# Gathering the later experts' rows with indirect transfers and combining the outputs in two one-pass products, in a two-layer encoder with 8 routed experts

## The reference

```python
logits = t @ w_router
top_vals, top_idx = lax.top_k(logits, 2)
top_w = softmax(top_vals)
combine = sum(one_hot(top_idx, 8) * top_w[..., None], axis=1)
for e in range(8):
    y = (silu(t @ w_gate[e]) * (t @ w_up[e])) @ w_down[e]   # 1024 -> 3584 -> 1024
    out = out + combine[:, e:e+1] * y
```

## Time and profile before

| | |
|---|---|
| median of 3 runs | 1826.73 us |
| the profiled execution, its own time | 1823.88 us |
| its span, first to last instruction | 1822.0 us |
| outside the span | 1.88 us |
| TensorE / VectorE / ScalarE / GpSimd busy | 97% / 77% / 65% / 1% of the span |
| the seven gathers of the loop, start of the first and of the last | 918.8 us, 1670.1 us |
| the experts, first product of step 0 to last down product | 807.9 us to 1807.0 us |

### The profile page before, as it was taken

How to read it: one execution, slowest core, us unless ns; L and a number is a source line. 1 busy time by engine, 2 the same in 40 slices (tenths; PEclk the granted TensorE clock), 3 DMA queues, 4 the chain that set the end, 5 groups by cost and what they waited for, 6 DMA issues and landing times.

```text
span 1822.0 us, 23915 instructions
## 1 busy us (share of the span) xinstructions
PE 1768.2 (97%) x8356; PEld 1449.6 (80%) x8356; DVE 1406.3 (77%) x1382; ACT 1177.0 (65%) x1242; POOL 20.2 (1%) x20
## 2 busy tenths in 40 slices
PE   7999999999999999989999999999999999999997
PEld 6777878888887778777888878878878888788785
DVE  7776876544577678769888889888888888898884
ACT  7555665434466556557777767677777777777772
POOL 0200000000002000000000000000000000000000
PEclk9999999999999999989999999999999999999999
DMA  7433345555454333668989989999999899899980
GB/s 278 162 116 116 116 155 188 189 185 185 157 196 139 116 128 127 259 251 342 374 333 358 370 318 371 349 341 378 344 346 372 329 362 366 322 371 346 343 323 25
DMA packets 67129, 475.79 MB, mean 261 GB/s; under 512 B 7793, under 2 KB 8049, under 8 KB 9969
## 3 DMA queue, kind: packets, MB, share of 16 engines
q1 hardware_dynamic: 67056, 474.86, 69.5%
HBM read 473.78 MB, written 1.05 MB: 261 GB/s over the span
## 4 chain that ended last, share of the span: by engine, by line
PE 87%; DVE 5%; ACT 3%; issue 1%; DVEq 1%; ACTq 1%; DMA 1%; SPq 0%
PE ps_proj L938 11%; PE ps_proj L942 11%; PE ps_proj L941 11%; PE ps_proj L538 7%; PE ps_proj L540 7%; PE ps_proj L541 7%; PE ps_score L938 6%; PE ps_score L941 6%; PE ps_score L942 6%; PE ps_ctx L532 3%; PE ps_score L532 2%; PE ps_trans L569 2%; PE ps_trans L532 1%; PE ps_score L538 1%; PE ps_score L541 1%
## 5 line engine op out<-in xcount | busy, mean ns | idle before, releaser
L2138 DVE TENSOR_TENSOR w_raw_r<-w_raw,hi 128x2048 fp32r<-128x2048 f32 x336 | 759.8, 2289 | 123.7 <-ACT hi L1450 107.5
L1450 ACT ACTIVATE hi<-w_raw 128x2048 fp32r<-128x2048 f32 x335 | 640.0, 1918 | 200.3 <-PE ps_score L942 77.7
L938 PE MATMUL ps_proj<-hi,he_hi 128*128 128x512 f32 x896 | 357.0, 398 | 0.6 <-DVE w_raw_r L2138 0.3
L942 PE MATMUL ps_proj<-w_raw_r,he_hi 128*128 128x512 f32 x896 | 349.4, 390 | 0.0
L941 PE MATMUL ps_proj<-hi,he_lo 128*128 128x512 f32 x896 | 349.2, 390 | 0.0
L1071 ACT ACTIVATE hi<-raw 128x2048 fp32r<-128x2048 f32 (+1 forms) x114 | 215.8, 1893 | 124.4 <-PE ps_proj L540 60.7
L1562 DVE TENSOR_TENSOR raw_r<-raw,hi 128x2048 fp32r<-128x2048 f32 (+1 forms) x114 | 257.1, 2265 | 34.2 <-ACT hi L1071 27.0
L538 PE MATMUL ps_proj<-hi,hT_hi 128*128 128x512 f32 (+2 forms) x496 | 198.7, 401 | 6.3 <-DVEq L1548 4.0
L938 PEld LDWEIGHTS ps_proj<-hi,he_hi 128*128 128x128 f32 x896 | 168.3, 188 | 36.4 <-issue 2.6
L942 PEld LDWEIGHTS ps_proj<-w_raw_r,he_hi 128*128 128x128 f32 x896 | 168.2, 188 | 36.2
L941 PEld LDWEIGHTS ps_proj<-hi,he_lo 128*128 128x128 f32 x896 | 168.5, 188 | 34.9 <-issue 1.7
(11 more groups left out here) (331 smaller groups left out, 2010.1 us busy)
## 6 DMA issues: line engine op xcount, KB each, us to landing
w_raw<-in_w_exp SPq DMA_DIRECT2D x336, 1024.0 KB, 4.8
raw<-in_w_pre SPq DMA_DIRECT2D x110, 1024.0 KB, 4.9
raw<-in_w_pre SPq DMA_DIRECT2D x4, 640.0 KB, 6.0
x_tok<-in_x_rows SPq DMA_DIRECT2D x2, 512.0 KB, 5.2
raw<-in_w_pre SPq DMA_DIRECT2D x2, 512.0 KB, 6.2
out_rows<-x_tok SPq DMA_DIRECT2D x1, 1024.0 KB, 4.7
grow<-in_ffn_row SPq DMA_DIRECT2D x1, 512.0 KB, 5.7
cst<-in_const SPq DMA_DIRECT2D x1, 344.0 KB, 8.5
```

Source lines behind the costliest of these rows:

```text
L938: m = nc.tensor.matmul(o, a_hi, w_h, start=first, stop=False)
L942: return nc.tensor.matmul(o, a_hi, w_l, start=False, stop=last)
L1450: A(w_hi[k % HS][:], w_raw[n], ACT.Copy).then_inc(gran_hi, 1)
L2138: V.tensor_tensor(w_low[k % WS], w_raw[k % WS], w_hi[k % HS][:].bitcast(F32), ALU.subtract)\
```

## The change

- The first expert's rows are gathered by products as before. SyncE also stores `htok` to a memory tensor `h_rows` (1 MB). For experts 1 to 7 GpSimd fetches 128 rows of 4 KB by an indirect transfer into `herow`, and TensorE transposes them (8 transposes, `turn_rows`) in step 6.
- The row numbers and weights by slot come from a new small product (`slot_columns`): `G` with `pair`, the weight and the row number of each token (2 columns, 2 float32 products). VectorE copies them to `idx` and `w_next`. It is done in step 4 for the next expert, and for the first expert after its step 0.
- The weight is applied to the expert's output: ScalarE writes `y_hi`, scaled and rounded to float32r, VectorE writes `y_lo`, the rest (`low_outputs`, in step 8 after the first `low`). `S` is now the transpose of `G`, in float32r. The combine is two float32r products, high and low, in place of one float32 product.
- `Gw` is gone; `one_weight` copies two columns instead.

SyncE:

```diff
+            sp.wait_ge(htok_ready, TT)
+            sp.dma_start(h_rows.rearrange("(t p) d -> p t d", p=P), htok[:]).then_inc(rows_stored, 16)
```

TensorE:

```diff
+            def turn_rows(number, bank_value):
+                pe.wait_ge(herow_in, number)
+                for half, bank in enumerate(("ctx", "trans1")):
+                    o = take(bank, bank_value(bank))
+                    for b in range(4):
+                        c = (half * 4 + b) * P
+                        m = nc.tensor.transpose(o[:, b * CAP:(b + 1) * CAP], herow[:, c:c + P], c_("ident"))
+                    m.then_inc(full[bank], 1)
+            def slot_columns(ready, value):
                 pe.wait_ge(weights_ready, ready)
                 o = take("proj2", value)
                 for t in range(TT):
+                    m = mm(o[:, 0:2], G[:, t], pair[:, t], t, TT)
+                m.then_inc(full["proj2"], 1)
+            def scatter_matrix(value):
+                o = take("proj2", value)
+                for t in range(TT):
-                    m = nc.tensor.transpose(o[:, t * P:(t + 1) * P], Gw[:, t], c_("ident"))
+                    m = nc.tensor.transpose(o[:, t * P:(t + 1) * P], G[:, t], c_("ident"))
                 m.then_inc(full["proj2"], 1)
             def combine(t, bank_value):
                 for half, bank in enumerate(("ctx", "trans1")):
                     o = take(bank, bank_value(bank))
-                    mm(o[:], S[:, t * P:(t + 1) * P], yrow[:, half * 512:(half + 1) * 512], 0, 1)\
-                        .then_inc(full[bank], 1)
+                    for n, y in enumerate((y_hi, y_lo)):
+                        m = mm(o[:], S[:, t * P:(t + 1) * P], y[:, half * 512:(half + 1) * 512], n, 2)
+                    m.then_inc(full[bank], 1)
...
+                    if s == 4 and not isinstance(e, int):
+                        slot_columns(along(2, rnd, EXPERTS, e, 1), bank_use("proj2", 2, rnd, e))
                     project(0, s, e)
...
                     if s == EXP_CHUNKS - 1 and not isinstance(e, int):
-                        gather(along(2, rnd, EXPERTS, e, 1), lambda bank: bank_use(bank, 1, rnd, e))
+                        turn_rows(along(16, rnd, 16 * EXPERTS, e, 16), lambda bank: bank_use(bank, 1, rnd, e))
...
                 step(0, 0)
+                if first_round(rnd):
+                    first_columns()
-                scatter_matrix(along(1, rnd, EXPERTS), bank_use("proj2", 0, rnd))
+                scatter_matrix(bank_use("proj2", 1, rnd))
                 step(1, 0)
```

ScalarE, in `outputs`:

```diff
-                        m = A(yrow[:, b * 512:(b + 1) * 512], o[:], ACT.Copy)
-                        if b:
-                            m.then_inc(y_ready, 1)
-                        act.drain().then_inc(free[f"score{b}"], 1)
+                        A(y_hi[:, b * 512:(b + 1) * 512], o[:], ACT.Identity, scale=w_now[:, 0:1])\
+                            .then_inc(y_hi_ready, 1)
```

VectorE:

```diff
             def one_weight(e):
                 for t in range(TT):
-                    m = V.tensor_scalar(Gw[:, t], c_("slot_no"), slots_of[:, t, bass.ds(e, 1)],
-                                        wt[:, t, bass.ds(e, 1)], ALU.is_equal, ALU.mult)
+                    m = V.tensor_copy(pair[:, t, 0:1], wt[:, t, bass.ds(e, 1)])
                 m.then_inc(weights_ready, 1)
+            def slot_columns(value):
+                o = fresh("proj2", value)
+                V.tensor_copy(idx[:], o[:, 1:2]).then_inc(idx_ready, 1)
+                V.tensor_copy(w_next[:], o[:, 0:1])
+                dve.drain().then_inc(free["proj2"], 1)
+            def weights_on():
+                V.tensor_copy(w_now[:], w_next[:])
+                dve.drain()
+            def low_outputs(number):
+                for b in range(2):
+                    dve.wait_ge(y_hi_ready, number(b + 1))
+                    half = slice(b * 512, (b + 1) * 512)
+                    m = V.scalar_tensor_tensor(y_lo[:, half], ps[f"score{b}"][:], w_now[:, 0:1],
+                                               y_hi[:, half].bitcast(F32), ALU.mult, ALU.subtract)
+                    if b:
+                        m.then_inc(y_ready, 1)
+                    dve.drain().then_inc(free[f"score{b}"], 1)
...
                     if s:
                         low(down0, e)
+                    if s == EXP_CHUNKS + 1:
+                        low_outputs(lambda n: along(n, rnd, 2 * EXPERTS, e, 2))
+                        weights_on()
+                    if s:
                         low(down0 + 1, e)
...
                     low(next0 + 1, e)
+                    if s == 4 and not isinstance(e, int):
+                        slot_columns(bank_use("proj2", 2, rnd, e))
...
                 step(0, 0)
+                if first_round(rnd):
+                    slot_columns(bank_use("proj2", 0, rnd))
+                    weights_on()
+                    dve.wait_ge(rows_stored, 16)
                 step(1, 0)
...
                 turned(EXP_CHUNKS - 1, last)
+                low_outputs(lambda n: along(n, rnd, 2 * EXPERTS, last, 2))
```

GpSimd:

```diff
+            def gather_rows(rnd, e):
+                pool.wait_ge(idx_ready, along(1, rnd, EXPERTS, e, 1))
+                pool.wait_ge(he_ready, along(0, rnd, 2 * EXPERTS, e, 2))
+                G_.indirect_dma_start(herow[:], None, h_rows, bass.IndirectOffsetOnAxis(ap=idx[:, 0:1], axis=0))\
+                    .then_inc(herow_in, 16)
+            pool.wait_ge(rows_stored, 16)
+            for e in range(1, EXPERTS):
+                gather_rows(0, e)
```

More of the change, by code:

```diff
@@ L48 @@
 CONST, CONST_COLS = columns(("ident", P), ("slope", HEADS), ("inv_freq", HALF), ("rope_g", DEPTH * 2 * ROPE),
-                            ("before", P), ("ones", P), ("slot_no", CAP), ("first_wins", EXPERTS))
+                            ("before", P), ("ones", P), ("slot_no", CAP), ("first_wins", EXPERTS), ("row_no", TT))
 GAIN, GAIN_COLS = columns(("attn", DB), ("ffn", DB), ("q_lat", QLB), ("kv_lat", KLB), ("qn", 1), ("kn", 1),
@@ L199, in first_gran @@
     return 6 * s - 2 if s else 0
-MOE_USES = dict(ctx=(24, 3), trans1=(24, 3), proj2=(8, 1), score0=(8, 1), score1=(8, 1))
+MOE_USES = dict(ctx=(24, 3), trans1=(24, 3), proj2=(16, 2), score0=(8, 1), score1=(8, 1))
 def bank_use(bank, k, rnd, e=0):
@@ L210, with build @@
 SBUF_AT = 16512
-def build(nc, x_rows, pos_row, pos_col, const, gains, lam_vecs, w_pre, ffn_row, w_router, w_exp, out):
+def build(nc, x_rows, pos_row, pos_col, const, gains, lam_vecs, w_pre, ffn_row, w_router, w_exp, out, h_rows):
     with ExitStack() as ctx:
@@ L303, in build @@
         grow = place("grow", [D], base + 32 * K)
-        yrow = place("yrow", [D], base + 32 * K)
+        y_hi = place("y_hi", [D], base + 32 * K, F32R)
         he_hi, he_lo = (place(n, [DB, CAP], base + at * K, F32R) for n, at in (("he_hi", 84), ("he_lo", 88)))
@@ L906, in route, with gather @@
                 mm(o[:, 2 * E:4 * E], ranks[:, 1], selb[:, 0:2 * E], 0, 1).then_inc(full["proj2"], 1)
-            def gather(value, bank_value):
+            def gather(bank_value):
                 pe.wait_ge(htok_ready, TT)
-                pe.wait_ge(gather_ready, value)
+                pe.wait_ge(gather_ready, 1)
                 for half, bank in enumerate(("ctx", "trans1")):
@@ L1493, in step @@
                     if s == EXP_CHUNKS + 1:
-                        scatter_matrix(bank_use("proj2", 1, rnd, e))
+                        scatter_matrix(bank_use("proj2", 3, rnd, e))
                     if s == EXP_CHUNKS - 1:
@@ L1504, in experts @@
                 step(0, 0)
-                scatter_matrix(bank_use("proj2", 0, rnd))
+                scatter_matrix(bank_use("proj2", 1, rnd))
                 step(1, 0)
@@ L2249, in _ @@
                 m.then_inc(rotated_q, 1)
+            def gather_rows(rnd, e):
[6 more added lines that the diff above has]
+                gather_rows(0, e)
+            pool.wait_ge(rounds_ready, 1)
+            n = pool.value_load(nrnd[0:1, 0:1], min_val=1, max_val=MAX_ROUNDS)
+            with pool.If(n > 1):
+                with pool.Fori(1, n) as rnd:
+                    for e in range(EXPERTS):
+                        gather_rows(rnd, e)
 def constants(f):
@@ L2347 @@
     out = nc.dram_tensor("out_rows", (T, D), F32, kind="ExternalOutput").ap()
-    build(nc, *args, out)
+    h_rows = nc.dram_tensor("h_rows", (T, D), F32).ap()
+    build(nc, *args, out, h_rows)
     r = run_bass_kernel_spmd(nc, [arrays], core_ids=[0])
```

31 lines of the change are left out of this document (25 added, 6 removed).

## The result

The changed kernel takes **1804.84 us** (median of 4 runs, 1804.76 to 1806.92); the kernel before beside it took 1826.50 us (4 runs, 1824.71 to 1827.22). The ratio is 0.9883, 95% interval 0.9871 to 0.9894: faster by 21.7 us. The forecast was 1811.5 us with a range of 1803.5 to 1821.5 us, of which 1806 to 1817 us was the forecast's own.

What follows compares the result with a forecast made beforehand. The prediction took TensorE to set the experts' time. Its terms summed to -15.2 us from the profiled 1823.88 us, giving 1808.7, plus 2.85 to the median: 1811.5 us, range 1803.5 to 1821.5 us (its own 1806 to 1817).

Steps and rivals of the forecast that it cites:

- The gather: In step 6 of the loop, eight transposes replace 32 instructions: 2.68 us gained, 7 times, -18.8 us.
- The combine: In step 8, four one-pass products per combine gain 0.81 us, 14 times in the loop: -11.3 us.
- Step 8's waits: TensorE's second combine waits for two banks that VectorE frees late: 0.7 us, 7 times, +4.9 us.
- Step 6: The shorter turn brings the next expert's gate product nearer to `he_lo`: +0.7 us for seven (0 to 3).
- The first expert's start: Between steps 0 and 1 TensorE waits 7.7 us for VectorE to read the columns, then half clock: +5.9 us.
- The end: After the last expert, y comes 1.0 us later and the last addition ends 0.3 us later: +0.3 us.
- What is hidden: The 1 MB store and the indirect transfers cost no time; the fetched rows have 33.7 us of cover.
- From execution to median: 2.85 us added, because the median of the runs stood that far above the profiled execution.
- (a): Milder handovers: no step 8 wait, no fall of the clock, no wait in step 6; 1804.3 us, 12%.
- (b): VectorE is held up 1.5 us more per expert beside GpSimd, in steps 4 and 5; 1822.0 us, 14%.
- (c): The combine's two products are not one-pass and gain nothing: 11.3 us more, 1822.8 us, 3%.
- (d): Indirect rows land after TensorE wants them in `turn_rows`; each microsecond beyond the cover costs 7; slower, 7%.

Runs made afterwards that it cites:

- e1: Changed kernel with the eight transposes of fetched rows made eight float32 products, each issued twice, the transfer kept: 1824.59 us, ratio 0.9997.
- e2: Changed kernel with the old float32 combine, without the second product and `low_outputs`: 1813.84 us, ratio 0.9935.
- e7: Changed kernel with `combined(0)` ahead of `low(next0+1)` in VectorE's step 8: 1802.71 us, ratio 0.9858.
- e3: Changed kernel with the first expert's columns moved behind step 1, so nothing waits for bank proj2: 1802.48 us, ratio 0.9872.
- e10: The kernel before, unedited, in one more profiled execution: 1829.02 us.
- e11: The changed kernel, unedited, run again: 1806.69 us, ratio 0.9878.
- e5: Changed kernel with the columns and the indirect transfer moved from step 4 to step 6 of each expert: 1854.85 us, ratio 1.0148.
- e6: Changed kernel with the columns and the indirect transfer moved from step 4 to step 5: 1805.20 us, ratio 0.9881.
- e9: The kernel before with one edit, VectorE's `turned(0)` two weight granules earlier in step 1: 1823.17 us, ratio 0.9975.
- e8: Changed kernel with the first expert's columns behind step 1, `combined(0)` earlier and `turned(0)` two granules earlier: 1795.10 us, ratio 0.9820.

## Why the prediction was right, step by step

The time lay 6.7 us under the forecast: in the stated range, 1.3 us above its lower end, but under the 1806 us where the forecast's own range began. So what was right is the mechanism and most of the terms. The sum's terms against what was measured:

- **The gather**, -2.68 us an expert: -2.70, and e1 gives it back (19.8 us with its noise, for 18.8). Right.
- **The combine**, -0.81 us: -0.79 for the first of the two; together with step 8's wait 6.4 us net were predicted, and e2's loop gives back 7.7.
- **The columns**, +0.45 us: 0.45 (877.48 to 878.16 us less one interval). Right.
- **Step 8's waits** were in the right place (bank trans1, VectorE late by its own order) and mis-sized: 0.7 us an expert was said, the holes come to 0.53 and 0.54 is what e7 wins back. The outputs' operations took 0.75 us as taken from the earlier trace rows.
- **Step 6**: 0.1 us an expert was said. The period leaves 0.05 for it: 2.70 + 0.79 + 0.26 - 0.45 is 3.30, measured 3.25. No run tried it alone.
- Together the loop gained 23.0 us where 21.4 were predicted.
- **The first expert's start**, +5.9 us: +5.3. The wait was 7.28 us for 7.7 predicted and the lost clock 1.4 for 1.6. The reading that a stand after small products is nearer to the earlier trace rows's half rate than to the 3.1 us that left the clock alone was right. What it took from those rows was too much, though: e3 and e10 show that the 3.1 us wait is no safe length. In e1, e2 and e11 the clock behind the 7.3 us wait cost about 3 us, in e5, e6 and e7 1.4 to 1.7, so the term is 5 to 7 us from run to run.
- **The end**, +0.3 us: +0.7; the second pair ran at half clock.
- **What is hidden** stayed hidden: TensorE waits neither for the store nor for a transfer, and the cover is 33.8 us (index read at 889.12 us, rows turned at 922.93) for 33.7 predicted. The full rate of 385 GB/s was read too low: stretches of 2 us show 418 GB/s, and 422 in the changed kernel; nothing hung on it.
- **From execution to median**, +2.85 us: this term missed most, and its reason was wrong. The prediction added to its forecast what the median of before stood above its profiled execution. The profiled kernel before was a lucky one, which kept its clock at two places where e10 lost 2.9 us each. The changed kernel has no clock to lose at 831 us, because its longer wait took that loss into the first expert's term; its median stands 0.1 us over its profiled execution. So the offset was in part added on top of a loss already counted. Only in part: the place at 178 us lies ahead of the experts and is left in both kernels, and in e11's series the changed kernel's median is 1806.69 us, 1.9 above that first profiled execution. How much of the 2.8 us is the chance of four runs is open.
- The rest of the miss lies outside the change: 1.5 us before step 0, which is chance, and 0.7 behind the last addition.

In sum the misses are 2.8 + 1.5 + 0.6 + 1.6 - 0.4 + 0.7 = 6.8 us (offset, before step 0, first expert, loop, end, behind the end; 6.7 unrounded).

**The rivals.** (a) named nearly the measured time, 1804.3 us, by a mechanism that didn't happen: the clock fell and the second combine waited. (b) did not happen: `low` takes 2290 ns on average as before, at most 2337, and GpSimd's instruction 0.94 us in six of seven cases (the first 2.69). (c) is out by the pitch of 0.23 us. (d) has its condition far off: the rows land 6.8 to 10.8 us after the issue, and the 33 us of cover are three times that. Its price of 7 us for each microsecond of lateness left out the clock: e5 pays 14 us of lost clock beside 33.0 us of stands. The Trainium skill's lock of GpSimd's descriptor writes by VectorE (SBUF — State Buffer, the "DVE blocks DMA" trap) is told there of VectorE's operations in a 2-port mode, such as copies of float32 within SBUF. This case does not test it: from 1000 to 1050 us VectorE is busy 43.4 us, and 39.5 of them are subtractions of two tensors. Beside these no transfer of the changed kernel took longer than 10.8 us. The 2.69 us of the first one is no such hold by what the runs show: it is 2.69 us in all ten traces with indirect transfers, also where e5 and e6 issue it at another time, and 0.94 in every later pass at the same place of the loop.

## What to carry to other kernels

Where one engine's instructions set the time, a change there is worth its pitch times its count, and the rest of the answer is which bank or buffer the shortened work now reaches too soon: here three handovers mended by the order of the work alone gave 9.7 us more. Not all of it is what the change gave back: the wait for `turned(0)` stood in the kernel before as well, and mended there alone (e9) it is worth 4.5 us. With that mend on both sides, and its own two handovers mended, the change is worth 28.1 us (e9 to e8), where it brought 21.7. A bank that the bound engine uses twice in a row, with a busy engine's read in between, is such a handover; put a step of work between the two uses (e3 moves the columns behind step 1), or the read ahead of a granule (e7). Before adding the distance between one profiled execution and the median to a forecast, look at where the clock fell in that execution: one trace is one draw of every such place.

## What the hardware showed unexpectedly

- The same wait of 3.1 us for the same instruction left the clock at 1.00 in one execution of the kernel before and at 0.50 in another (e10), and in e3. Behind it TensorE worked about 6 us at half rate, 2.9 us lost. A wait of 3.3 us at 178 us, in the attention, which neither the change nor an edit touches, stands in all thirteen traces: four kept the clock behind it, nine lost 1.4 to 3.0 us.
- How long the half rate lasts behind the same wait of 7.3 us differs too: 1.4 us lost in the changed kernel, 3.0 in e11, the same kernel.
- Of the differences between runs of one kernel a large part is this: 6.3 us more lost clock came with a span 5.2 us longer. Less its lost clock, the kernel before has spans of 1816.9 and 1815.8 us (e10), and the changed kernel, which lost 7.6 and 9.9 us, of 1795.3 and 1795.8 us (e11): what the change is worth, 20.0 to 21.6 us, does not hang on that draw. What decides the draw was not tried.
- An indirect transfer of 128 rows of 4 KB lands in 7.0 us beside the full weight stream and in 4.3 us where that stream has all but stopped; beside the stream the medians of the other runs are 6.8 to 9.4 us. The weights' own transfers of 1 MB land in 6.7 us (median) in the changed kernel and 4.8 in the kernel before, at nearly the same rate (371 and 362 GB/s). That follows the loop's pace and not the indirect transfers: e1 and e5, with these transfers and a loop no faster than before, have 4.9 and 4.8 us, e2, in between, 5.4, and the six other traces at the changed kernel's pace or a faster one 5.7 to 6.7. It costs nothing here; no run varied it alone.
